# The first pair's rows fetched for four tiles ahead of the last tile's routing, the last tile by a one-hot product, and four planes of expert three in other rooms

## What is computed

```python
x = x + jnp.dot(merged, w_out)
h = rmsnorm(x, g_ffn)                       # 544 tokens, 1024 wide
gl = h @ w_group + b_group                  # 4 groups, the best one is taken
el = (h @ w_router + b_router)[group]       # 8 experts in it, the best two are taken
# every expert e of 32, for its tokens:
y = (silu(h @ w_gate[e]) * (h @ w_up[e])) @ w_down[e]
x = x + weighted sum of a token's two y
x = x + sigmoid(rmsnorm(x, g_ple) @ w_ple_gate) * (p @ w_ple)
out = rmsnorm(x, g_final)
```

## Time and profile before

| | us |
|---|---|
| median of three runs | 1022.1 (1021.7 to 1022.69) |
| the profiled execution's own time | 1020.0 |
| its span | 1017.9 |
| PE busy | 911.9 (90%) |
| DVE busy | 379.0 (37%) |
| ACT busy | 258.3 (25%) |
| POOL busy | 141.3 (14%) |

### The profile page before, as it was taken

How to read it: one execution, slowest core, us unless ns; L and a number is a source line. 1 busy time by engine, 2 the same in 40 slices (tenths; PEclk the granted TensorE clock), 3 DMA queues, 4 the chain that set the end, 5 groups by cost and what they waited for, 6 DMA issues and landing times.

```text
span 1017.9 us, 14245 instructions
## 1 busy us (share of the span) xinstructions
PE 911.9 (90%) x5747; PEld 585.0 (57%) x5750; DVE 379.0 (37%) x973; ACT 258.3 (25%) x525; POOL 141.3 (14%) x146
## 2 busy tenths in 40 slices
PE   7999999989999999989999988788887787888996
PEld 7969995557999997973333322222232222334775
DVE  4279998754233354362111110100110101113696
ACT  6354328664231342231000000000000000002542
POOL 2705432122110000001111101001101011000000
PEclk9999999999999999998999999999999999999998
DMA  8860602005734406487999999999999999997601
GB/s 268 115 162 1 208 1 63 1 2 164 220 77 110 119 2 269 150 311 298 423 423 428 426 429 425 426 427 426 427 425 427 426 427 427 428 422 317 259 22 68
DMA packets 61096, 265.88 MB, mean 261 GB/s; under 512 B 11118, under 2 KB 36094, under 8 KB 47312
## 3 DMA queue, kind: packets, MB, share of 16 engines
q1 hardware_dynamic: 55120, 253.08, 65.1%
q0 software_dynamic: 5296, 9.79, 2.7%
q10 hardware_dynamic: 624, 2.23, 0.6%
HBM read 256.09 MB, written 16.85 MB: 268 GB/s over the span
## 4 chain that ended last, share of the span: by engine, by line
PE 61%; DMA 29%; DVE 4%; issue 3%; ACT 2%; SPq 1%; POOL 0%; DVEq 0%; POOLq 0%; ACTq 0%
DMA arena<-in_w_up 26%; PE ps L1205 14%; PE ps L1373 12%; PE ps L1060 5%; PE ps L1238 4%; PE ps L1526 4%; PE ps L1398 4%; PE ps L1006 3%; PE ps L981 2%; PE ps L1150 2%; PE ps L1129 1%; PE ps L1099 1%; PE ps L943 1%; PE ps L1267 1%; PE ps L936 1%
## 5 line engine op out<-in xcount | busy, mean ns | idle before, releaser
L1373 PE MATMUL ps<-arena,hT 128*64 128x512 f32 x960 | 231.7, 635 | 37.9 <-DMA arena<-in_w_up 37.8
L1373 PEld LDWEIGHTS ps<-arena,hT 128*64 128x64 f32 x960 | 70.1, 139 | 196.6 <-issue 146.9
L2342 DVE TENSOR_TENSOR xf<-xf,ps 128x256 f32<-128x256 f32 x32 | 13.5, 421 | 398.1 <-ACT xf L1819 375.5
L1205 PE MATMUL ps<-arena_merge,arena_merge 128*128 128x256 f32 x624 | 99.7, 287 | 0.0
L891 POOL DMA_INDIRECT expert_rows<-xf,arena x32 | 32.0, 1001 | 422.9 <-ACT xf L1823 396.9
L1398 PE MATMUL ps<-arena,xf 128*64 128x512 f32 x336 | 76.7, 597 | 14.8 <-DVE xf L2345 13.4
L1205 PEld LDWEIGHTS ps<-arena_merge,arena_merge 128*128 128x128 f32 x624 | 87.5, 188 | 0.0
L1205 PE MATMUL ps<-xf_merge,arena_merge 128*128 128x256 f32 x480 | 82.0, 288 | 0.0
L1819 ACT ACTIVATE xf<-ps 128x256 f32<-128x256 f32 x30 | 11.5, 384 | 255.0 <-PE ps L1373 255.0
L1205 PEld LDWEIGHTS ps<-xf_merge,arena_merge 128*128 128x128 f32 x480 | 69.3, 188 | 0.0
L1823 ACT ACTIVATE xf<-ps 128x512 f32<-128x512 f32 x30 | 17.9, 597 | 160.9 <-PE ps L1398 160.9
(11 more groups left out here) (323 smaller groups left out, 1306.2 us busy)
## 6 DMA issues: line engine op xcount, KB each, us to landing
arena<-in_w_gate SPq DMA_DIRECT2D x30, 2048.0 KB, 30.5
arena<-in_w_up SPq DMA_DIRECT2D x30, 2048.0 KB, 37.3
arena<-in_w_down SPq DMA_DIRECT2D x11, 2048.0 KB, 36.0
arena<-in_w_down SPq DMA_DIRECT2D x20, 1024.0 KB, 30.9
hT<-in_w_down SPq DMA_DIRECT2D x10, 2048.0 KB, 36.5
arena<-in_w_in SPq DMA_DIRECT2D x10, 1024.0 KB, 6.5
arena<-in_w_in SPq DMA_DIRECT2D x3, 2048.0 KB, 11.1
arena<-in_w_gate SPq DMA_DIRECT2D x8, 512.0 KB, 9.0
```

Source lines behind the costliest of these rows:

```text
L1205: mm = pe.matmul(w[:, 2 * lo_t:lo_t + hi_t], rounded(st[:, c, cols]), rounded(mv[:, c, lo_t:hi_t]), start=c == 0 and k == 0, stop=c == pla ...
L1373: mm = pe.matmul(ps[g * BLK:(g + 1) * BLK, 2 + s, :], xsT[:, c, col:col + BLK], expert_columns(k, slice(0, 2), c, g), start=c == 0, stop=c ...
```

## The change

The order of rows in `normed_rows` becomes tiles 0, 1, 2, 4, 3 (`FIRST_ROW`, `stored_rows`), so that the first 416 rows are four tiles. The table of rows is closed twice: once behind the fourth tile in order (`index(3)`), in columns 0 to 31 of its bank, and for the last tile alone in columns 32 to 63. From the first, DVE makes only the first pair's fetch list; POOL clears `xs[0]` and fetches rows of those four tiles. The last tile's share of the first pair is a product on PE: `first_rows` adds `x_nat` of tile 3 times a scaled one-hot matrix (`last_tile_hot`) to the turned rows in the same bank. `ranks(3)` moves ahead of the last quarter of the projection, `keep_busy(2)` stands ahead of `ranks(4)`, and `keep_busy(3)` and `keep_busy(1)` behind the table are gone. DVE's `turned_half` moves ahead of the scatter lists.

Four planes of expert 3 (its first four, of gate and of up) are loaded to four rooms outside its place: the room of `g_fin`, that of tile 4 in `x_nat`, and two in the arena. Two of these loads stand behind the second down load over `x_nat`, two behind `xsT_full` and `rt_exp_in`. The up planes 0 to 3 of expert 1 move behind SP's wait for `xs_in[0]`. Since `g_fin` and tile 4 of `x_nat` are overwritten, `g_final` is loaded near the end instead of the beginning, and tile 4 is loaded back from `normed_rows`, where it stands scaled, with one factor more in the sums.

The diff, cut to its core:

```diff
+        def load_room(c):
+            for m in range(2):
+                load(ROOMS[c][:, m], A[('w_gate', 'w_up')[m]][0, PLACES].rearrange("(p c) n -> p c n", c=KD)[:, c], gu_in[0])
+        sp.wait_ge(gu_in[0], 32)
+        load_room(0)
+        load_room(1)
...
         sp.wait_ge(part_used, 2)
-        load_planes(1, 1, 0, 2)
-        load_planes(1, 1, 2, 4)
         sp.wait_ge(rows_full, TILES)
         sp.wait_ge(xs_in[0], 16)
+        for c in range(0, KD, 2):
+            load_planes(1, 1, c, c + 2)
         load_planes(2, 1, 5, 8)
-        load_planes(1, 1, 4, 6)
-        load_planes(1, 1, 6, 8)
...
+        sp.wait_ge(xsT_full, 1)
         load_dn_over_rows(3)
+        sp.wait_ge(rt_exp_in, 1)
+        load_room(2)
+        load_room(3)
...
+        sp.wait_ge(gu_done, 1)
+        for m in range(2):
+            load(w_gu[0][:, m, len(ROOMS):], A[('w_gate', 'w_up')[m]][0, PLACES].rearrange(
+                "(p c) n -> p c n", c=KD)[:, len(ROOMS):], gu_in[0])
...
-        load(x_nat[:, 0:4, :], xn_d[0:NP].rearrange("(t p) n -> p t n", p=P), x_in[0])
+        load(x_nat[:, 0:3, :], xn_d[0:3 * P].rearrange("(t p) n -> p t n", p=P), x_in[0])
+        for t in range(3, TILES):
+            load(x_nat[0:ROWS[t], t, :], xn_d[stored_rows(t)], x_in[0])
+        load(g_fin[:, :], A['g_final'].unsqueeze(0).to_broadcast([P, D]), consts_in)
...
+        link(pool.memset(xs[0], 0.0))
         pool.wait_ge(index_ready, 1)
-        for p in range(3):
+        gather(xs[0], gather_of[:, 0:1], xs_in[0], xn_d[0:NT - P], early_bound)
+        pool.wait_ge(sample_stored, 32)
+        pool.wait_ge(index_ready, 2)
+        for p in range(1, 3):
             gather(xs[p], gather_of[:, p:p + 1], xs_in[p])
...
+        def first_rows(lo, hi, last):
+            w = wide(0).rearrange("p (c t) -> p c t", c=KD)
+            for c in range(lo, hi):
+                st, mv = (x_nat[:, 3, c:D:KD], first_hot.rearrange("p s n -> p (s n)")) if last else (xs[0][:, c:D:KD], ident[:, :])
+                mm = pe.matmul(w[:, c, :], st, mv, start=not last and c % (KD // 2) == 0, stop=last and c % (KD // 2) == KD // 2 - 1)
+            return mm
...
         logits(4)
+        keep_busy(2)
         ranks(4)
+        pe.wait_ge(xs_in[0], 16)
+        first_rows(0, KD, False)
+        pe.wait_ge(place_ready, TILES)
+        first_rows(0, KD // 2, True).then_inc(turn_full, 1)
         index(4)
+        first_rows(KD // 2, KD, True).then_inc(xsT_full, 1)
...
-        keep_busy(3)
-        pe.wait_ge(index_ready, 3)
+        pe.wait_ge(index_ready, 4)
...
-        pe.wait_ge(xs_in[0], 16)
-        rows_turned(0, 0, KD // 2).then_inc(turn_full, 1)
-        rows_turned(0, KD // 2, KD).then_inc(xsT_full, 1)
-        keep_busy(1)
...
+            if i == 0:
+                link(dve.tensor_tensor(v[0:NS, 1:2], v[0:NS, 1:2], nrm[0:NS, UNIT + 4:UNIT + 5], ALU.mult))
```

More of the change, by code:

```diff
@@ L1347, in _ @@
         mm.then_inc(index_done, 1)
-        pe.wait_ge(turn_out, TILES)
-        def keep_busy(n):
-            for _ in range(n):
-                pe.matmul(ps[:, 2, :], ident[:, :], g_fin[:, 0:512], start=True, stop=True)
-        keep_busy(3)
-        pe.wait_ge(index_ready, 3)
+        pe.wait_ge(index_ready, 4)
         def rows_turned(k, lo=0, hi=KD):
@@ L1409, in pair @@
                     pe.wait_ge(xsT_ready, p + 1)
[L1410 to L1411 removed]
+                pe.wait_ge(gu_in[k], gu_count(e, k, use))
+                gate_up(s, k, s * BLK, ROOMS if body == 0 and e == PLACES else []).then_inc(gu_done, 1)
                 if s == 0:
```

136 lines of the change are left out of this document (88 added, 48 removed).

## The result

The changed kernel takes 1027.3 us (median of 6 runs, 1026.6 to 1031.2) against 1021.9 us for the kernel before on the same chip (6 runs, 1020.8 to 1024.2): a ratio of 1.0062, 95% interval 1.0049 to 1.0074. The ratio is estimated from all runs and is not the quotient of the two medians, which is 1.0053. The kernel is slower by 5.4 us in the median (6.1 in the mean), where 2.4 us faster was forecast, and the time lies outside the forecast range of 1017.6 to 1023.6. The profiled execution took 1027.1 us with a span of 1025.4, 7.5 us more than the span of before (1017.9).

What follows compares the result with a forecast made beforehand. The weight stream, full from 490 to 930 us, was taken as the bound, its start set by PE's way to expert 4's issue: -4.1 + 1.5 + 0.2 = -2.4 us, from 1022.1 to 1019.7 us, range 1017.6 to 1023.6.

Steps and rivals of the forecast that it cites:

- the two limits: Before expert 4's weights: the stream's backlog and PE's way to the issue; after the change PE's decides, stream 4.1 us earlier.
- The fetch: First pair's early fetch by POOL: starts at 451.5, rows land 4.5 us later at 456.0, where SP resumes instead of 464.8.
- the rooms: Places for early planes of expert 3: worth next to nothing, since without them the stream would end level with PE's limit.
- The late rows: Rival: second pair's fetch lands late in a full queue and PE stalls; +4.2 us, 1026.3 us; chance 0.13.
- the size argument: Against the late rows: if fetch delay goes with the size of queued loads' rows, the second pair lands in 7.2 us.
- 1.5 us for tile 0's results: At the end: g_fin and tile 4 put 41 KB more on a slow DMA engine ahead of these results; bounds 0 and 1.5.
- the DVE operation's 0.2: In the norm behind the experts: one more linked DVE operation and its wait cost 0.2 us on the chain.
- I take 0.25: Price in us of one 128-column float32 product in first_rows, taken from the logits' row; first gate_up then 4.1 us earlier.
- The upper bound: Dearest price of such a product: 0.51 us, half the 512-column filler; 3.5 us worse, leaving 0.6 us of gain.
- the clock takes part of it: Rival: fallen clock slows fillers, ranks(4) and first_rows; start 1.0 to 2.2 us later, 1020.7 to 1021.9 us; chance 0.27.
- 20.3 us behind the start: Expert 4's weights are issued 20.3 us after the first gate_up starts, before and after the change.
- The lost start with its costs: Rival: the earlier start does not reach the end, leaving only the end's costs; 1022.1 to 1023.8 us; chance 0.10.

Runs made afterwards that it cites:

- a_side: a_hold_end with ScalarE copying tile 3's rows side by side, the last tile's one-hot products taking weights from that copy: 1016.8 us, 0.9961 of the kernel before.
- a_hold_end: Changed kernel with table load hidden, g_fin's load later, fetched rows turned in transpose mode ahead of ranks(4), fillers where PE waits: 1019.1 us, 0.9968 of the kernel before.
- a_gfin: Changed kernel with g_fin's load moved behind the loads of the experts' rows in SP's queue: 1026.4 us, 1.0060 of the kernel before.
- a_table: Changed kernel with ScalarE's wait for the stored row tiles moved ahead of its exponentials: 1026.2 us, 1.0034 of the kernel before.
- a_norooms: Changed kernel without the rooms, all planes of expert 3 loaded behind the first gate_up: 1028.6 us, 1.0064 of the kernel before.
- a_probe2: Product-price probe: fetched rows times the router's 36 columns, last tile's products with tile 3's turned rows as weight: 0.50 and 0.51 us a product, clock 0.50.
- a_probe3: Product-price probe: fetched rows' products summed in one PSUM place, last tile's with a 64-column weight: 0.51 and 0.31 us a product.
- a_probe: Product-price probe: fetched rows' products stream 64 columns, last tile's take neighbouring weights: 0.50 us a product at clock 1.00, 0.51 at 0.50.

## Why the prediction was wrong

**What held.** The picture of the two limits: the stream ran dry ahead of expert 4 and PE's way decided; a_side and a_hold_end follow it to within some tenths. The fetch: forecast at 451.5 and landed at 456.0, it was issued at 451.81, landed 3.9 us later, and SP went on at 455.75. The picks: forecast 456.95, read 456.87. The one-hot matrix was hidden, the rooms worth nothing (two kernels). The late rows did not come: the later fetches (pairs 1 and 2) took up to 7.5 us under small loads, and 7.2 was the size argument's answer. At the end, 1.5 us for tile 0's results measured 1.9, and the DVE operation's 0.2 is there.

**What failed, in the forecast's order.**

- *"I take 0.25"* for a product, from the logits, "because the weight load is what they share". This is the step that failed: the term was mis-sized, 16 products at 0.51 instead of 0.25, 4.1 us, the whole forecast gain. The weight load was not shared: it took 191 ns in the logits and 334 in `first_rows`. The nearest row was near in the width of the weight and not in how it lies in SBUF: the logits read theirs side by side, `first_rows` at a step of 32 bytes. The upper bound, half of the 512-column filler, gave the right number by accident, from a row without a step.
- *The fillers.* The rival "the clock takes part of it" came: 1.8 us each in the changed kernel's profile, `ranks(4)` 1.2 us late. It was priced at 1.0 to 2.2 us, which is right; it had a chance of 0.27.
- *"20.3 us behind the start"*, taken as a constant of the kernel, was 23.2. Two things sat in it. The first `gate_up` may run in part at half clock, 1.6 us here and up to 2.9 in other runs (10.29 us in a_gfin). And the diff moved a wait of ScalarE ahead of its first pair; I priced the DMAs and PE's instructions that the change moved, but not this one line, behind which a table load of 1.28 us lost its cover. That term was missing altogether.
- *The end.* The direct cost was right, but the sum stopped there. PE waits for these results, and behind the longer wait its clock was lower: 1.6 us more. The same mechanism stood in the late rows' rival (a stall, then 9.05 us instead of 7.42) and was not carried to the end.
- *The range.* From the forecast's product to the dear bound it counted 3.5 us, and the clock was another 2.2, and both add on one chain. The range took them one at a time, reached 1023.6 and missed. (The lost start with its costs is 1022.1 + 1.5 + 0.2 = 1023.8, not 1023.6.) By its own numbers the dear product left 0.6 us of the start's gain; with the 1.7 us of the end that was already a loss, and the clock came on top. The 3.5 is itself too small: 16 products at 0.51, worked through the same steps, end at 466.1 us and put the first `gate_up` at 466.9, so nothing of the gain was left.

Summed from these terms: -4.1 forecast, +4.1 products, +1.2 fillers, +1.6 `gate_up`, +1.3 table, +1.9 and +1.6 at the end, +0.2, -0.5: +7.3, where the spans differ by 7.5.

## What to carry to other kernels

Price an operation of a new form by the nearest row in how its operands lie in memory, not only in their sizes, and where two bounded terms lie on the same chain add their bad ends before you set the range. When work is taken from waiting on DMA and given to PE, look for everything that hid under the old wait (a table load, a lower clock) and for the PE that now idles elsewhere. A load issued into an "idle" share near the end can delay the small transfer that everyone waits for.

## What the runs showed of the hardware

- A float32 product with a weight of 128 columns costs 0.29 us when the weight's elements are neighbours and 0.51 to 0.54 when they are 32 bytes apart, at a granted clock of 1.00; at 0.50 the first costs 0.51 and the second 0.50 to 0.57. A 64-column weight with the step costs 0.31. One load of such a weight took 334 ns with the step and 191 without it, but 193 with the step in a turn.
- In the changed kernel PE ran products from 458.5 to 466.9 us at a granted clock of 1.00. Behind a gap of 0.98 us the clock fell to 0.50 as `gate_up` began, at 468.2, and `gate_up` took 9.04 us. The gap alone doesn't decide: a_table, a_norooms, a_probe2 and a_probe3 had one of 0.97 to 1.02 us and took 7.42. With a filler in it, and 0.23 to 0.24 us left, all three kernels took 7.42. In a_probe the clock fell at about 463.9, in the midst of products, with no gap of PE ahead since 453.6.
- With a load of 512 KB issued at 927 us, 19 us ahead of the transfer that the chain waits for, that transfer took 6.51 to 7.37 us in seven profiles, and 5.18 to 6.42 in those without; in the pairs that differ in little else it was 1.3 to 1.9 us longer.
- Fetches of 4 KB rows by POOL landed after 3.9 us where the DMA engines moved 161 GB/s (452 to 456 us) and after 7.5 where they moved 403 GB/s (466 to 474 us), under loads of 2 to 6 KB in a row.
